# GpSimd's modulation products as four 128x256 tensor_scalar multiplications instead of one 128x1024 tensor_tensor by a broadcast column

## What is computed

```python
sc_c = jax.nn.silu(c)
sc_ctx = jax.nn.silu(c_ctx)
for l in range(DEPTH):
    m = (sc_c @ w_mod[l] + b_mod[l])[:, None, :]
    sh1, s1, g1, sh2, s2, g2 = jnp.split(m, 6, axis=-1)
    mc = sc_ctx @ w_mod[l] + b_mod[l]
    ...
    h = modulate(rmsnorm_2(x, norm_g[l, 0]), sh1, s1)
```

## Time and profile before

| | |
|---|---|
| median of 3 runs | 3065.79 us (3062.63 to 3070.58) |
| the profiled execution | 3065.65 us, span 3063.7 us |
| PE busy (matrix products) | 2829.8 us, 92% |
| DVE busy | 1619.5 us, 53% |
| ACT busy | 1050.7 us, 34% |
| POOL busy | 704.3 us, 23% |
| the modulation on POOL, layer 0 | from 48.6 to 495.4 us; PE uses it from 739.9 us |
| the modulation on POOL, layer 1 | from 1984.0 to 2314.9 us |
| line 608, the instruction to which the change applies | 112 times, 1946 ns each, 217.9 us |

### The profile page before, as it was taken

One profiled execution on the slowest core, in us unless ns is written; L12 is line 12 of the kernel. 1 busy time (PEld: TensorE's weight loads), 2 busy tenths in 40 slices (PEclk: granted clock), 3 DMA queues, 4 the chain that ended last, 5 costly groups with the idle time before them and its releaser, 6 DMA issues. The chain is left out here.

```text
span 3063.7 us, 31137 instructions
## 1 busy us (share of the span) xinstructions
PE 2829.8 (92%) x12266; PEld 2161.4 (71%) x12266; DVE 1619.5 (53%) x2428; ACT 1050.7 (34%) x1606; POOL 704.3 (23%) x532
## 2 busy tenths in 40 slices
PE   6998869999998888999999978879999999999998
PEld 5886657886976336888878853357788766678886
DVE  4453894654233563747554254457664489543333
ACT  3344323333233344434245233323222311432223
POOL 3996784000000000000000000099992010000000
PEclk9999989998998899999998968789999899999999
DMA  4544344322222002233323310045553211123331
GB/s 147 159 144 138 97 143 127 98 88 66 63 90 69 1 1 69 83 96 96 93 86 97 94 35 1 14 134 163 171 166 116 62 55 55 49 81 98 97 96 48
DMA packets 284807, 274.67 MB, mean 90 GB/s; under 512 B 13473, under 2 KB 268727, under 8 KB 284407
## 3 DMA queue, kind: packets, MB, share of 16 engines
q1 hardware_dynamic: 266759, 210.47, 22.2%
q0 software_dynamic: 16864, 62.17, 6.3%
q10 hardware_dynamic: 1040, 0.07, 0.0%
HBM read 270.56 MB, written 2.10 MB: 89 GB/s over the span
## 5 line engine op out<-in xcount | busy, mean ns | idle before, releaser
L455 DVE TENSOR_TENSOR w_lo<-raw,w_hi 128x1024 fp32r<-128x1024 f32 x396 | 571.1, 1447 | 936.9 <-ACT w_hi L450 936.6
L1792 PE MATMUL G<-H_hi,w_hi 128*128 128x512 f32 (+1 forms) x1984 | 798.7, 403 | 51.7 <-DVE H_lo L341 18.9
L450 ACT ACTIVATE w_hi<-raw 128x1024 fp32r<-128x1024 f32 x396 | 417.2, 1057 | 1139.2 <-PE G L1792 1012.6
L1792 PE MATMUL G<-H_lo,w_hi 128*128 128x512 f32 (+1 forms) x1984 | 780.3, 393 | 0.0
L1792 PE MATMUL G<-H_hi,w_lo 128*128 128x512 f32 (+1 forms) x1984 | 779.9, 393 | 0.0
L1792 PEld LDWEIGHTS G<-H_hi,w_hi 128*128 128x128 f32 x1984 | 380.3, 192 | 149.6 <-issue 42.9
L1792 PEld LDWEIGHTS G<-H_lo,w_hi 128*128 128x128 f32 x1984 | 380.3, 192 | 84.3 <-issue 7.7
L1792 PEld LDWEIGHTS G<-H_hi,w_lo 128*128 128x128 f32 x1984 | 379.4, 191 | 79.8
L1792 PE MATMUL G<-hid_hi,w_hi 128*128 128x512 f32 x864 | 344.4, 399 | 31.4 <-DVE hid_lo L558 23.9
L1792 PE MATMUL G<-hid_lo,w_hi 128*128 128x512 f32 x864 | 339.2, 393 | 0.0
L1792 PE MATMUL G<-hid_hi,w_lo 128*128 128x512 f32 x864 | 338.9, 392 | 0.0
(11 more groups left out here) (284 smaller groups left out, 3229.8 us busy)
## 6 DMA issues: line engine op xcount, KB each, us to landing
raw<-in_w_ff SPq DMA_DIRECT2D x128, 512.0 KB
mod_w<-in_w_mod POOLq DMA_DIRECT2D x112, 512.0 KB, 3.9
raw<-in_ffn_w_up SPq DMA_DIRECT2D x176, 256.0 KB
raw<-in_ffn_w_down SPq DMA_DIRECT2D x40, 512.0 KB
raw<-in_w_in SPq DMA_DIRECT2D x28, 512.0 KB
raw<-in_mlstm_w_in SPq DMA_DIRECT2D x24, 512.0 KB
raw<-in_kv_w SPq DMA_DIRECT2D x16, 512.0 KB
raw<-in_fox_w_qg SPq DMA_DIRECT2D x16, 512.0 KB
```

Of the source, the lines that this page charges most:

```text
L450: act.activation(w_hi[:, j, :], raw[:, j, :], ACT.Copy).then_inc(hi_done, 1)
L455: dve.tensor_tensor(w_lo[:, j, :], raw[:, j, :], w_hi[:, j, :], ALU.subtract).then_inc(lo_done, 1)
L1792: mm = pe.matmul(G[:, 2 * p + m, 0:n], lw[:, k, ms], rh[:, t, 0:n], start=(t == 0 and q == 0), stop=(t == st["ktiles"] - 1 and q == 2), sk ...
```

## The change

The instruction of line 608 multiplied all four row blocks (128x1024) in one `tensor_tensor`, whose second operand was four numbers per partition, each read 256 times (`to_broadcast`). Now each row block is multiplied by its own `tensor_scalar` of 128x256, whose factor is one number per partition. There is no wait between the four; only the last one raises the semaphore on which line 609 (now 611) waits. All other lines stay as they are and move down by two in the file. Per half POOL has six or seven arithmetic instructions instead of three or four.

```diff
                     for half in range(2):
                         w = mod_w[:, half]
                         pool.wait_ge(mod_landed[half], i * 16 + 16 * (lands[0] + 1))
-                        col = cs[:, 8 * vec + 4 * half:8 * vec + 4 * half + 4].unsqueeze(2).to_broadcast([P, 4, MCH])
-                        step(pool.tensor_tensor(w, w, col, ALU.mult), 3 * half + 1)
+                        for k in range(4):
+                            c = 8 * vec + 4 * half + k
+                            one = pool.tensor_scalar(w[:, k], w[:, k], cs[:, c:c + 1], None, ALU.mult)
+                        step(one, 3 * half + 1)
                         step(pool.tensor_tensor(w[:, 0:2], w[:, 0:2], w[:, 2:4], ALU.add), 3 * half + 2)
```

## The result

The changed kernel takes 3070.98 us (median of 20 runs, 3069.71 to 3078.93) against 3065.72 us for the kernel before (median of 20 runs). The ratio of the means is 1.0023, 95% interval 1.0013 to 1.0034. It is slower by 5 to 7 us, clear of noise, and about inside the 0.3% that I had called "within". The forecast was 3058 us.

A forecast was written before the change was run, and what follows sets the result against it. The prediction took DVE, held up by POOL's instructions, to bound stage f0_up0, by 40 us of idle PE. 3065.65 - 6 (that stage) - 1 (the fill near 2050 us) = 3058.7, given as 3058 us; range 3029 to 3085.

The forecast's parts named there:

- within: A measured time that about 0.3% (9.2 us) can't tell from no change; chance 0.36.
- What bounds the kernel: In stage f0_up0 DVE is the bound, held behind POOL's instructions, by 40 us of idle PE.
- The length of a tensor_scalar: In POOL's modulation, 0.39 us for each 128x256 instruction; a block of four 1.6 us, between 1.1 and 3.2.
- No turns within the block: In f0_up0 DVE gets no turn between the four instructions, so a block shorter by 0.3 us saves 6 us.
- The turns' price: In f0_up0, if DVE gets turns between the four, each added turn costs 0.1 us; 37 us saved in eight groups.
- That rival: DVE gets a turn between the four: 37 us less in f0_up0, 7 lost in f0_up1, 6 at fill; 3030 us, chance 0.28.
- The cover at the end of layer 1: POOL ends layer 1 58 us before PE asks; gone if POOL slows by 1.2 us a half over 48 halves.
- the two rivals: DVE gets turns between the four (3030 us, chance 0.28); tensor_scalars slower than before (3085 us, chance 0.22).
- turns, but long instructions: DVE gets turns between the four but POOL's instructions are long: no clear change in time; chance 0.03.
- The likeliest case: A block of 1.1 to 2.0 us and no turns: 6 us saved in f0_up0, 1 at fill; 3058 us, chance 0.45.
- the turns' case: DVE gets a turn between POOL's four instructions, mainly freeing f0_up0; 3030 us, chance 0.28.
- the slow case: A block over 1.91 us makes DVE wait longer in f0_up0; at 2.7 us it costs 19 us: 3085, chance 0.22.

## Why the prediction was wrong

**What bounds the kernel: right.** Ffn 0 was bound by DVE and DVE by POOL's instructions. With DVE freed, 36 of the 40 us of waits went.

**The length of a tensor_scalar: wrong, and outside both bounds.** I took 0.39 us, between 0.26 and 0.74; it is 0.91, and starts are 0.90 apart. The upper bound was the two-operand sum, on the argument that one stream can't cost more than two. It costs more: 2.5 ns a column against 2.1 for the sum. A row of another operation bounds nothing if the reason for it is only that it seems to do more. The Trainium skill's rule that one-input operations of GpSimd are roughly line-rate (GPSIMD Engine Reference, section 4.1, Engine selection) doesn't hold for this operation: the block takes 3.7 us, where the prediction's estimate by that page was 1.1.

**No turns within the block: wrong for the tensor_scalar, partly right for the tensor_tensor.** I read from the missing turn between the transfer and line 608 that instructions with no wait between them would go as one. The tensor_tensor quarters did so when DVE was already waiting. The tensor_scalars don't hold DVE long in any case, since they give the path free 0.3 to 0.5 us after their start. Nor does the transfer ahead of them: before, 27 of 28 two-operand DVE instructions that started while POOL issued a transfer were held to about the end of line 608, 2.1 us in the mean; in the changed kernel 23 such instructions waited 0.06 us in the mean and 0.21 at most. That second part I hadn't considered: I equated what DVE waits with what POOL's instruction lasts. The Trainium skill, SBUF — State Buffer, section Who interferes with whom, calls the shared ports an exclusive lock and says of VectorE's 2-port modes that whoever issues first has them for the whole instruction; the prediction applied that to two-input instructions. The rows nearly agree for POOL's tensor_tensor (held for 1.77 of 1.91 us) and not for its tensor_scalar (0.98 of 2.86).

**The turns' price: near in size, partly by luck.** That rival's 37 us in ffn 0 stand against 36 us of waits gone and 40.4 us at the start of layer 1's run. But it was worked out with pieces of 0.4 us that hold DVE to their end. With pieces of 0.91 us the same working (a turn costs the piece less 0.3) gives 0.6 for each added turn, 5.8 us of waits a group instead of 7.8, some 16 us less in eight groups, as an estimate. The 37 us came out because a piece of 0.91 us holds the path for only 0.3 to 0.5. Its 7 us of loss in `f0_up1`, from POOL's work spilling over, came as one wait of 1.8 us more: POOL works until 609 us, and PE waits for line 558 for 4.2 us in that stage instead of 2.3. Its 6 us at the fill near 2050 us were too few for the 18 us that came up to 2315 us. Of these, 9 are waits for H_lo (14.9 us before, 6.0 now) and 4 the waits for line 1465, which are gone; the rest was not traced one by one, but the granted clock from 2050 to 2075 us is 1.00 where it was 0.79.

**The cover at the end of layer 1: right in kind, wrong in size.** I had named the 58 us, and 1.2 us a half as the point where they are gone. The half grew by 2.06 us, because the block alone grew by 1.71. And I had not worked the two rivals together: "turns, but long instructions" has a chance of 0.03 and no sum. The 58 us are counted from PE's old arrival. A kernel in which DVE gets its turns is also one in which PE arrives sooner, by 18 us within layer 1's run, and POOL is held up more, by 0.35 us a half. 99 us of lengthening less 58 of cover plus 18 of earlier arrival is 59: the wait that was measured.

**The forecast.** The likeliest case was a sum of two wrong steps with opposite signs, the block's length and the missing turns. The measured time lies in the range of 3029 to 3085 only because the turns' case (3030) and the slow case (3085) both happened and cancelled.

## What to carry to other kernels

An engine with time to spare may be made slower on purpose if that frees another's path; then find the place where its result is needed, and count its cover from the new arrival of the one that waits. Where a change acts in several stages, each stage may want its own form: here the one line gave 1.9% with a form for each layer, 1.4% with the tensor_tensor quarters in both and nothing with the tensor_scalars in both. And an operation that no row shows has no upper bound: if the sign hangs on it, say so in the chances.

## What the runs showed of the hardware

- On POOL a float32 `tensor_scalar` multiplication of 128x256 takes 0.91 us and of 128x1024 2.86 us; a `tensor_tensor` by a broadcast column takes 0.58 and 1.91 us. A factor from memory costs 0.08 us more than a constant.
- How long DVE is held isn't how long POOL's instruction lasts. A two-operand DVE instruction got to work 0.98 us into a POOL tensor_scalar of 2.86 us and 0.3 to 0.5 us into one of 0.91 us, but 1.77 us into a tensor_tensor of 1.91 us (reckoned from starts, lengths and DVE's bare times).
- Two-operand DVE instructions that started while POOL issued a transfer (0.79 us) were held to about the end of the tensor_tensor behind it, 2.1 us in the mean; with 128x256 tensor_scalars behind it they waited 0.06 us in the mean, with the 128x1024 one 0.97.
- Four tensor_tensors with no wait between them ran as one block of 2.32 us past a waiting DVE; a semaphore wait between them gave DVE a turn each time. Why the four go as one was not tried.
